# Seven lower parts ahead of the last gate's multiply, two output blocks side by side, and a later place for the second norm's sum

## What is computed

```python
merged = jnp.zeros_like(x)
for i, y_i in enumerate((y_a, y_b, y_c, y_d)):
    gate = jax.nn.sigmoid(gate_raw[..., i * D_MODEL:(i + 1) * D_MODEL])
    merged = merged + gate * (y_i.astype(adt) @ w['w_branch'][i])
x = x + merged @ w['w_out']
h2 = rmsnorm(x, w['norm2_g'])
up = h2 @ w['ffn_up']
```

## Time and profile before

| | us |
|---|---|
| median of 3 runs (lowest, highest) | 1955.31 (1949.58, 1956.50) |
| profiled execution, its own time | 1957.76 |
| its span, first to last instruction | 1956.0 |
| mean granted TensorE clock | 0.985 of full speed |

### The profile page before, as it was taken

The page is one execution under the profiler, slowest core; times in us unless marked ns, Lnnn a source line. Parts: engine busy times, 40 slices in busy tenths (PEclk is TensorE's granted clock), DMA queues, the critical chain, the costliest instruction groups (busy, mean ns, idle before and its releaser), DMA issues.

```text
span 1956.0 us, 29880 instructions
## 1 busy us (share of the span) xinstructions
PE 1868.4 (96%) x11562; PEld 1793.5 (92%) x11562; DVE 894.5 (46%) x1359; ACT 412.0 (21%) x591; POOL 584.2 (30%) x532
## 2 busy tenths in 40 slices
PE   5889999999999998999999999999999999999996
PEld 4889978888899878999999989999999999999986
DVE  5764244326523334222241155555555555555555
ACT  5210033423311113011121132112111111111213
POOL 2323210022233323343332224324323432432420
PEclk9989999999999999999999999999999999999999
DMA  4121120022132212321332311111111111111202
GB/s 124 45 52 37 46 88 23 12 82 66 39 94 67 72 58 77 92 72 54 92 88 67 97 33 44 51 37 54 43 32 54 53 33 43 54 43 32 64 10 98
DMA packets 156098, 113.44 MB, mean 58 GB/s; under 512 B 10742, under 2 KB 146651, under 8 KB 155990
## 3 DMA queue, kind: packets, MB, share of 16 engines
q1 hardware_dynamic: 153084, 102.61, 18.3%
q10 hardware_dynamic: 2940, 9.81, 1.3%
HBM read 95.37 MB, written 16.99 MB: 57 GB/s over the span
## 4 chain that ended last, share of the span: by engine, by line
PE 88%; DVE 7%; ACT 2%; issue 1%; DMA 1%; ACTq 0%; SPq 0%; POOL 0%; DVEq 0%; POOLq 0%
PE ps L1929 20%; PE ps L1935 19%; PE ps L1932 19%; PE ps L2364 4%; PE pt L2464 4%; PE pt L2466 4%; PE pt L2465 4%; PE ps L2136 2%; PE ps L2097 2%; PE ps L2404 1%; PE pt L2122 1%; DVE ext L1833 1%; PE ps L1986 0%; PE ps L2243 0%; PE ps L1987 0%
## 5 line engine op out<-in xcount | busy, mean ns | idle before, releaser
L1929 PE MATMUL ps<-h_hi,w_hi 128*128 128x352 f32 x2472 | 551.7, 332 | 18.8 <-POOL w_lo L877 6.0
L1932 PE MATMUL ps<-h_lo,w_hi 128*128 128x352 f32 x2472 | 536.4, 325 | 0.0
L1935 PE MATMUL ps<-h_hi,w_lo 128*128 128x352 f32 x2472 | 536.3, 325 | 0.0
L1929 PEld LDWEIGHTS ps<-h_hi,w_hi 128*128 128x128 f32 x2472 | 420.1, 191 | 30.7 <-issue 16.9
L1935 PEld LDWEIGHTS ps<-h_hi,w_lo 128*128 128x128 f32 x2472 | 426.8, 189 | 0.0
L1932 PEld LDWEIGHTS ps<-h_lo,w_hi 128*128 128x128 f32 x2472 | 424.7, 190 | 0.0
L870 POOL TENSOR_TENSOR mark<-eps 128x1 f32<-128x1 f32 x159 | 53.3, 335 | 1113.3 <-PE ps L1935 555.2
L877 POOL TENSOR_TENSOR w_lo<-w_raw,w_hi 128x1024 fp32r<-128x1024 f32 x127 | 333.4, 2626 | 10.2
L1867 DVE TENSOR_TENSOR y_all<-y_all,pt 128x352 f32<-128x352 f32 x264 | 137.6, 521 | 113.5 <-PE pt L2466 110.6
L2464 PE MATMUL pt<-act_hi,w_hi 128*128 128x352 f32 x528 | 172.1, 326 | 8.1 <-DVE y_all L1867 6.9
L2466 PE MATMUL pt<-act_hi,w_lo 128*128 128x352 f32 x528 | 170.7, 323 | 0.0
(11 more groups left out here) (335 smaller groups left out, 1795.3 us busy)
## 6 DMA issues: line engine op xcount, KB each, us to landing
w_raw<-in_w_in SPq DMA_DIRECT2D x52, 512.0 KB, 4.3
w_raw<-in_ffn_up SPq DMA_DIRECT2D x44, 512.0 KB, 3.8
w_raw<-in_ffn_down SPq DMA_DIRECT2D x22, 512.0 KB, 3.5
gates_dram<-y_all ACTq DMA_DIRECT2D x16, 528.0 KB, 2.7
cst<-gates_dram SPq DMA_DIRECT2D x16, 528.0 KB, 3.6
x_tok<-in_x_prompt SPq DMA_DIRECT2D x8, 512.0 KB, 3.9
bw_raw<-in_w_branch SPq DMA_DIRECT2D x32, 128.0 KB, 3.5
w_raw<-in_w_out SPq DMA_DIRECT2D x8, 512.0 KB, 4.7
```

Of the source, the lines that this page charges most:

```text
L1929: mm(dst[:, c, 0:CH], f_hi[n][:, k, :], h_hi[:, k, tok], start=k == 0, stop=False)
L1932: mm(dst[:, c, 0:CH], f_hi[n][:, k, :], h_lo[:, k, tok], start=False, stop=False)
L1935: last = mm(dst[:, c, 0:CH], f_lo[n][:, k, :], h_hi[:, k, tok], start=False, stop=k == KD - 1)
```

## The change

Three things change. (1) On VectorE the last turn of the merge (j = 7) is taken out of the loop and rearranged: after the multiply of branch 2 come the lower parts 0 to 6 of `merged`, then the add of branch 2, the multiply and the add of branch 3, and the lower part 7. (2) On TensorE output blocks 0 and 1 are made side by side: steps 0 to 6 of block 0 into `ps[0]`, steps 0 to 6 of block 1 into `ps[1]`, then step 7 and the residual of block 0, and step 7 and the residual of block 1. (3) `EARLY_H2` goes from 2 to 5, so that five upper and lower parts of the second norm stand ahead of the copy, the square and the adding of block 7, and the sum of squares on TensorE goes from ahead of step 5 to ahead of step 7. SyncE's and GpSimd's programs are the same text.

```diff
-    EARLY_H2 = 2
+    EARLY_H2 = 5
...
-        with dve.Fori(1, KD) as j:
+        with dve.Fori(1, KD - 1) as j:
             od.enter(j, 1)
             merge(j)
-        od.leave(KD - 1)
-
-        for k in range(KD):
-            dve.wait_ge(m_hi_done, k + 1)
-            od.run(v.tensor_tensor(h_lo[:, k, :], merged[:, k, :], h_hi[:, k, :].bitcast(F32), ALU.subtract), m_split)
+        od.leave(KD - 2)
+
+        merge(KD - 1, range(2))
+        gated(KD - 1, 2)
+        for k in range(KD - 1):
+            merged_lower(k)
+        summed(KD - 1, 2)
+        merge(KD - 1, [3])
+        merged_lower(KD - 1)
...
-        def product(dst, n, between=None):
+        def product(dst, n, between=None, ks=range(KD)):
...
-            for k in range(KD):
+            for k in ks:
...
+        def first_out_blocks():
+
+            for s in range(2):
+                n = W4 + s
+                pe.wait_ge(w_split, n + 1)
+                pe.wait_ge(br_read, 4 * KD - 1 + s)
+                stairs = {k: [lambda k=k: pe.wait_ge(m_split, k + 1)] for k in range(KD - 1)} if s == 0 else None
+                product(ps[s], n % 2, stairs, range(KD - 1))
+            pe.wait_ge(m_split, KD)
+            for s in range(2):
+                product(ps[s], (W4 + s) % 2, None, [KD - 1]).then_inc(merged_used, 1)
+                add_residual(0, s)
...
-                    stairs[5].append(sum_of_squares)
+                    stairs[KD - 1].append(sum_of_squares)
```

More of the change, by code:

```diff
@@ L1779, in _, with gated, summed, merge @@
             od.run(v.tensor_tensor(y_lo[:, b, :], y_all[:, b, :], y_hi[:, b, :].bitcast(F32), ALU.subtract), y_split)
[L1781 to L1788, removed]
+        def gated(j, q):
+            dst = merged[:, bass.ds(j, 1), :].rearrange("p o n -> p (o n)")
+            dve.wait_ge(br_full, j * 4 + (q + 1))
+            dve.wait_ge(sg_ready, j * 4 + (q + 1))
+            gate = sg[:, :] if q % 2 == 0 else sgl
+            out = dst if q == 0 else gate
+            od.run(v.tensor_tensor(in_chunks(out), in_chunks(gate), chunked((1, 0, 0, 1)[q]), ALU.mult), br_read)
+        def summed(j, q):
+            dst = merged[:, bass.ds(j, 1), :].rearrange("p o n -> p (o n)")
+            od.run(v.tensor_tensor(dst, dst, sg[:, :] if q % 2 == 0 else sgl, ALU.add), merged_done)
+        def merge(j, qs=range(4)):
+            for q in qs:
+                gated(j, q)
                 if q > 0:
-                    od.run(v.tensor_tensor(dst, dst, gate, ALU.add), merged_done)
+                    summed(j, q)
+        def merged_lower(k):
+            dve.wait_ge(m_hi_done, k + 1)
+            od.run(v.tensor_tensor(h_lo[:, k, :], merged[:, k, :], h_hi[:, k, :].bitcast(F32), ALU.subtract), m_split)
         od.peel()
         merge(0)
-        with dve.Fori(1, KD) as j:
+        with dve.Fori(1, KD - 1) as j:
             od.enter(j, 1)
             merge(j)
-        od.leave(KD - 1)
-        for k in range(KD):
-            dve.wait_ge(m_hi_done, k + 1)
-            od.run(v.tensor_tensor(h_lo[:, k, :], merged[:, k, :], h_hi[:, k, :].bitcast(F32), ALU.subtract), m_split)
+        od.leave(KD - 2)
[6 more added lines that the diff above has]
+        merged_lower(KD - 1)
         def sum_squares(i, blocks=range(2)):
@@ L2384, in _, with add_residual @@
             branch(j, 3)
[L2387 to L2396, removed]
+        def add_residual(i, s):
             pe.wait_ge(ld_res[s], i * 32 + 32)
@@ L2408, in out_block @@
             last.then_inc(wo_full, 1)
-        for s in range(2):
-            out_block(0, s)
+        def out_block(i, s):
+            n = W4 + s
+            pe.wait_ge(w_split, i * 2 + (n + 1))
+            pe.wait_ge(wo_read, i * 2 + (s - 1))
+            product(ps[s], n % 2).then_inc(merged_used, 1)
+            add_residual(i, s)
+        def first_out_blocks():
+            for s in range(2):
+                n = W4 + s
+                pe.wait_ge(w_split, n + 1)
[6 more added lines that the diff above has]
+                add_residual(0, s)
+        first_out_blocks()
         pe.wait_ge(ld_fh, 16)
```

## The result

The changed kernel takes 1964.72 us in the median of 6 runs (1958.25 to 1967.36), the kernel before 1955.44 us in the median of 6 (1949.58 to 1956.50): a ratio of 1.0056, with a 95% interval of 1.0035 to 1.0078. Two longer series (12 runs each, further down) gave 1.0036 (1.0020 to 1.0052) and 1.0046 (1.0030 to 1.0062). By these three ratios the change costs some 7 to 11 us; 1961.6 was forecast, +6.3.

A forecast was written before the change was run, and what follows sets the result against it. The prediction took TensorE, busy 96% of the span, as the bound, so only its waits and slow clock could change. Output blocks +6.8 and norm -0.5 gave +6.3 us on the median 1955.31: 1961.6 us, range 1954 to 1967.

The forecast's parts named there:

- What bounds it: TensorE, busy 96%; in the touched stretch, waits of 4.2 and 3.9 us for VectorE's lower parts, with slow clock behind.
- Part 1, the late count: Merge's end: 4.2 us wait goes, but last add ends 8.70 us later, delaying block 1's weight load and split.
- Part 2, the wait: Output blocks side by side: TensorE idles 11.2 us for block 1's split weights; with part 1 +6.8 us (5.6 to 9.7).
- Part 3, the norm: Second norm: short waits for lower parts and a new 1.25 us wait for the square root; -0.5 us taken.
- Weights in time: Rival, output blocks: block 1's weights are split when TensorE asks at 1022.55; sum -7.7, 1947.6 us; chance 0.08.
- The clock that falls again and again: Rival, second norm: four short waits keep the clock at half; norm +6.0, sum +12.8, 1968.1 us; chance 0.10.
- The unblocked norm: Rival, second norm: GpSimd's subtraction doesn't come between lower parts; -3.5 there, sum +3.3, 1958.6 us; chance 0.10.
- The sum: Whole kernel: output blocks +6.8 and norm -0.5 give +6.3 us, 1961.6 us on the median's scale; chance 0.72.

The follow-up runs named there:

- Two longer series: The changed kernel again without edit, 12 runs each, against the kernel before: 1962.16 us, ratio 1.0036, and 1962.37 us, ratio 1.0046.
- merge-only kernel: Changed kernel with the second norm as before (`EARLY_H2 = 2`, sum of squares ahead of step 5): 1963.64 us, ratio 1.0032 to the kernel before.
- the unblocked order: Changed kernel with early second `w_out` load, GpSimd's third up block split held back, sum of squares ahead of step 6: 1941.80 us, ratio 0.9945.
- the two runs with early weights and a late split: Changed kernel, second `w_out` load early, GpSimd's third up block split held back; sum ahead of step 7: 1946.78 us; ahead of step 6: 1941.80 us.

## Why the prediction was right, and where it was off

**What bounds it.** Right. Both waits named were the ones that the edits touch, and the 4.2 us wait went as worked out: TensorE starts block 0 with the end of the branch product and doesn't wait for lower parts 1 to 6.

**Part 1, the late count.** Right to a tenth. From the start of branch 2's multiply to the last add 14.16 us were forecast, 14.18 measured. From the add to GpSimd's start 6.20 was taken from before; 6.6, 6.1 and 6.4 were measured, and 7.9 with the norm as before: the landing of that load varies by nearly 2 us. The split took 3.6 as forecast. The edit to SyncE's queue alone removed the wait, so this cause is shown.

**Part 2, the wait.** 11.2 us forecast, 11.3, 10.7 and 11.1 measured. The step that was off is the price of the half clock behind it. I took 2.85 us, the price behind the 4.2 us wait, and twice that as the upper end. Against the stretch without any wait (29.4) the three profiles of the changed kernel lost 42.1 - 11.3 - 29.4 = 1.4, 1.6 and 1.4 us, and the merge-only kernel 2.2. So the output blocks cost +5.8, not +6.8; the lower end of 1.6 was nearer.

**Part 3, the norm.** The waits were forecast at 0.45, 1.8, 1.0 and 1.25 us for lower parts 2, 3 and 5 and for the square root; the lists show 1.65, 0.82 and 1.19 for the last three, and step 2 is some 0.3 us later than where GpSimd's split is held back. The clock held (1.00 in the window above), and the stretch fell by 0.6 us for -0.5 forecast. But the second profile of before puts that gain in another light: without slow clock the old order takes 20.3 us, 0.9 less than the new order. The new order isn't shorter; it spares a slow-clock stretch that the old one mostly pays (21.8 in five of the six profiles with the old order, 20.3 in the sixth). In the times it is worth nothing that can be told: ratio 1.0004.

Why the waits come was right too. In the changed kernel the first five lower parts take 9.40 us for the 6.74 of the unblocked order, beside a subtraction of GpSimd that is stretched as in the earlier trace rows:

```profile
1138.76 9.40 DVE L1840 SCALAR_TENSOR_TENSOR h_lo<-y_all,pv,h_hi 128x1056 fp32r<-128x1056 f32 x5 [8.33 <-ACT h_hi L1298]
1148.19 1.26 DVE L1826 TENSOR_TENSOR ssq<-ssq,sq 128x1056 f32<-128x1056 f32 x1
1149.49 4.03 DVE L1840 SCALAR_TENSOR_TENSOR h_lo<-y_all,pv,h_hi 128x1056 fp32r<-128x1056 f32 x3
```

```profile
1142.42 3.27 POOL L877 TENSOR_TENSOR w_lo<-w_raw,w_hi 128x1024 fp32r<-128x1024 f32 x1
```

The Trainium skill, SBUF — State Buffer, section "SBUF: two separate sides", has VectorE and GpSimd lock each other out of a shared port pair for whole instructions, where the VectorE operation has two inputs in SBUF (here `y_all` and `h_hi`) and GpSimd's reads SBUF too. Holding GpSimd's split back gave 21.2 - 18.8 = 2.4 us, which agrees with it. TensorE's rows of the changed kernel, from the last residual on, with the four waits in brackets (lower parts 0, 3 and 5, and the root) and the sum of squares at 1153.84, 4.6 us ahead of the second up product:

```profile
1137.22 2.73 PE L2413 MATMUL ps<-cst,x_res 128*128 128x128 f32 x22
1140.23 0.73 PE L1946 MATMUL ps<-h_hi,w_hi 128*128 128x352 f32 x3 [0.27 <-DVE h_lo L1840]
1146.86 0.75 PE L1946 MATMUL ps<-h_hi,w_hi 128*128 128x352 f32 x3 [1.65 <-DVE h_lo L1840]
1150.86 0.75 PE L1946 MATMUL ps<-h_hi,w_hi 128*128 128x352 f32 x3 [0.82 <-DVE h_lo L1840]
1153.84 1.94 PE L2459 MATMUL ps<-ssq,ones_m 128*128 128x352 f32 x6
1158.44 0.72 PE L1946 MATMUL ps<-h_hi,w_hi 128*128 128x352 f32 x3 [1.19 <-ACT cst L1300]
```

**The rivals.** Weights in time: not so, and its price was right where the load was moved (7.5 us in the profile against 7.2 and 0.5). The clock that falls again and again: no, four waits of up to 1.65 us left it at 1.00. The Trainium skill, TensorE: Matmul & The Clock Gate, section "HAM oscillation — how this bites in real kernels", describes that course for longer waits that come again and again; no run here shows it. The unblocked norm was made, not met: held back, with the sum where the change puts it, it took 18.8 against the 18.3 that -3.5 meant.

**The sum.** That +6.3 came so near is in part luck. The first pair of profiles shows +5.8 - 0.6 = +5.2 for the two terms of the sum, and -1.5 us in the middle, for which the sum had no term: it left the clock behind the transposes as before without saying so. Together that is +3.7. The times, +7 to +11, hold a rest beyond the forecast that no profile shows. The two misses have opposite signs and partly cancel.

**What stays open.** The profiles show +3.4 to +5.3 us for the changed stretches (151.1 to 151.4 against 146.15 to 147.7), the three series of times +7 to +11. The second series of the kernel before narrows that: against its 1955.69, the changed kernel's 1962.37 beside it is +6.7. The profiled executions of the changed kernel lie mostly under its medians (1958.76, 1962.77 and 1959.30 against 1964.72, 1962.16 and 1962.37), those of before above (1957.76 against 1955.44, 1957.58 against 1955.69). That slow clock fell on the other executions more often would fit, but only their mean clock is known, and a mean also counts the clock inside an idle wait, where it costs nothing (0.50 from 1022 to 1029 in the 11.28 us wait); what separates them was not shown.

## What to carry to other kernels

Moving work of one engine ahead delays what it is moved past, so look for every count that the delayed instructions raise and for every queue that waits for it in order: here a weight load stood behind a wait that had nothing to do with it. Interleaving two products moves the need for the second's inputs to the front, and takes away the cover that hid their load. Two edits that cost little or nothing alone (+1.0 us and nothing in the stretch) can cost +5.8 together, so check them together too.

## What the runs showed of the hardware that was not expected

The half clock did not cost more behind a longer wait: 1.4 to 2.2 us behind 10.7 to 12.6 us, against 36.2 - 4.2 - 29.4 = 2.6 us behind 4.2 us. And the same wait of 3.6 us in the same kernel was followed by half clock in one profile (0.52) and by full clock in another (1.00), a difference of 1.5 us in one place. The Trainium skill, TensorE: Matmul & The Clock Gate, section "What's actually happening", calls the count of matmuls that one kernel makes before its clock rises run-variable; these two profiles differ by more than that, since in the second the clock did not fall at all.

Behind the history transposes the clock varied too, with the time from these to the last residual at 89.6, 88.2 or 86.6 us in unchanged code. Repeats of one kernel agreed there (88.2 three times, 89.6 or 89.7 twice), but runs with the same program up to the end of the stretch did not: the merge alone took 86.7 against 88.2, the two runs with early weights and a late split 89.6 and 88.1. A gain of that size in one profile is not yet a gain of the kernel.
